# A gate projection in products of 256 moving columns in place of 512, in a fused two-layer block on one Trainium2 core

## The chip, the core and the metric

The kernel runs on one core of a Trainium2 chip. The core has a matrix engine (TensorE, PE in the profile; its weight loads are shown apart as PEld), a vector engine (VectorE, DVE), a scalar engine (ScalarE, ACT), GpSimd (POOL) and SyncE (SP), which issues the transfers from the chip's memory. A product of TensorE has a stationary operand (the weights in the array, up to 128x128), which a weight load brings in, and a moving operand, whose columns stream past it; the result is added up in a PSUM bank. The metric is the device time of one execution in microseconds (us), lower is better.

## What is computed

A first layer block (a convolution branch, a gated recurrence and a per-layer embedding with a gate) is followed by a second one (dilated attention, retention). All inputs are float32; there are 512 tokens of 2048 features. The part that the change concerns is the gate near the end of the first block:

```python
def first_block(x, p, norm_mix_g, w_in, ..., w_ple_gate, w_ple_proj, final_norm_g):
...
        m = jax.nn.sigmoid(ga) * (ya @ w_a_out[i]) + jax.nn.sigmoid(gb) * (yb @ w_b_out[i])
        x = x + m @ w_o[i]

        gate = jax.nn.sigmoid(rmsnorm(x, ple_norm_g[i]) @ w_ple_gate[i])
        x = x + gate * (p[i] @ w_ple_proj[i])

    return rmsnorm(x, final_norm_g)
```

`w_ple_gate` is 2048 x 2048, and x is 512 x 2048. The second block starts with another norm and its own input projection.

## The kernel before, in words

**Layout.** Activations are kept transposed, features on the 128 partitions and the 512 tokens along the row, as 16 k-tiles of 128 x 512. Every dense projection computes, for each group of 512 output features, four output tiles of 128 features x 512 tokens, each in a PSUM bank of its own (128 x 512 float32 fills a bank).

**Three products per tile pair.** To keep float32 accuracy with the reduced type `fp32r`, both operands are split in a high and a low part: WH and WL for the weights, XH and XL for the activations. Each k-tile of each output tile takes three products into the same bank: XH with WH, XL with WH, and XH with WL. In the names of the profile, `bank<-XL,WH` is the product with moving XL and stationary WH. So the stationary operand of the first two products is the same. ScalarE makes the high part from the loaded weights (line 395), VectorE the low part (line 418), units of two k-tiles at a time. SyncE loads the units (`load_unit`, line 453) through four buffers `RAW`; `WH` and `WL` have three buffers each.

**The program `pe`.** It walks through all projections in a fixed order and calls `pe_dense` for each group; the products come from line 366. The gate projection, `("gate", g)` for g in 0 to 3, has 16 k-tiles in each group. It comes behind `("proj", g)` (moving PH and PL) and ahead of `("qr", 0)`, the first projection of the second block. With `fed=True` the products of the first k-tile are ordered by part (XH,WH of all four tiles, then XL,WH, then XH,WL), since the activations are just being made; the others go three by three.

**Signals.** Every engine's program is written out with semaphores. The first product of a tile waits for its weights, its activations, and the bank's last reader; the last product of a tile signals `dense`, on which ScalarE waits for the sigmoid of the gate (line 2111, `GT<-bank`). VectorE multiplies with the projected embedding and adds to x (lines 2508 and 2512). The last product of a unit signals too, and frees the weights' buffers for line 395.

**Other work on TensorE that the argument uses.** Line 467 sums with a matrix of ones, in full float32; lines 472 and 473 do it in `fp32r` with two products; line 1943 sums four pieces of 128 columns in full float32. Lines 782 and 798 are small products of the recurrence, of 32 stationary columns. In the last output group, line 366 has products of 384 moving columns (`cols=EARLY`), with the names KEPT_H and KEPT_L for kept weights.

Of the kernel before, what the change touches and what calls it, by code (L numbers as in the profile page):

```python
# [107 lines left out]
def idle(n):  # L108
    for _ in range(n):
        yield  # L110
# [84 lines left out]
for _name, _w, _r, _nk, _c in GROUPS:  # L195
    FIRST[_name] = len(UNITS)
    for _k in range(0, _nk, 2):
        _row = _r + (_k + 8) % 16 * 128 if _name[0] == "out" else _r + _k * 128
        UNITS.append((_w, _row, _c))
EARLY, LATE = slice(0, 384), slice(384, 512)  # L200
NKEPT = 5
KEPT = range(FIRST["out", 3], FIRST["out", 3] + NKEPT)
LASTU = range(FIRST["out", 3], len(UNITS))
# [21 lines left out]
def build(nc, xT, pT, vec, logits, cst, masks, ident, w_in, w_a, w_b, w_o, w_gate, w_proj,  # L225
# [6 lines left out]
    def sb(name, shape, dt, at):  # L232
        return nc.alloc_sbuf_tensor_at(name, [128] + shape, dt, offset=base + at)
# [4 lines left out]
    XH = sb("XH", [16, 512], F32R, 40960)  # L238
    XL = sb("XL", [16, 512], F32R, 73728)
# [10 lines left out]
    W0 = C0 + 3680 + 4 * NVEC  # L250
    KEPT_H = sb("KEPT_H", [NKEPT, 2, 512], F32R, W0 + 32768)
    KEPT_L = sb("KEPT_L", [NKEPT, 2, 512], F32R, W0 + 53248)
    GB = sb("GB", [2, 512], F32, W0 + 90112)
# [24 lines left out]
    bank = [nc.alloc_psum_tensor(f"bank{i}", [128, 512], F32) for i in range(8)]  # L278
# [46 lines left out]

    pe_turns, act_turns, dve_turns, sp_turns = Turns(), Turns(), Turns(), Turns()

    def pe_dense(name, xh, xl, ready, swap=False, kmap=None, fed=False, cols=slice(0, 512)):
        nk = NK[name]
        mine = take(4, 0, NDENSE)  # L330
        banks[name] = mine
        gone = [held[b] for b in mine]
        for i, b in enumerate(mine):
            held[b] = (free_by(name), (name, i))
        for k in range(nk):
            n = FIRST[name] + k // 2
            wh, wl = high_of(n), low_of(n)
            if fed and k == 0:
                work = [(0, i, (j,)) for j in range(3) for i in range(4)]
            elif fed and k == 1:  # L340
                work = [(1, i, (0, 1, 2)) for i in range(4)]
            else:
                work = [(k - k % 2 + j, i + k % 2 * 2, (0, 1, 2)) for i in range(2) for j in range(2)]
            for q, i, parts in work:
                kk = kmap[q] if kmap else q
                b = mine[i]
                c = slice(i * 128, i * 128 + 128)
                if swap:
                    pairs = [(xh[:, kk, c], wh[:, q % 2]), (xl[:, kk, c], wh[:, q % 2]),
                             (xh[:, kk, c], wl[:, q % 2])]  # L350
                else:
                    pairs = [(wh[:, q % 2, c], xh[:, kk]), (wh[:, q % 2, c], xl[:, kk]),
                             (wl[:, q % 2, c], xh[:, kk])]
                for j in parts:
                    l, r = pairs[j]
                    if j == 0:
                        T.wait_ge(hi, (yield hi, n if n or q else "first"))
                        T.wait_ge(xhi, (yield xhi, (ready, kk)))
                        if q == 0 and gone[i]:
                            T.wait_ge(gone[i][0], (yield gone[i]))  # L360
                    if j == 1:
                        T.wait_ge(xlo, (yield xlo, (ready, kk)))
                    if j == 2:
                        T.wait_ge(lo, (yield lo, n if n or q else "first"))
                    first, final = q == 0 and j == 0, q == nk - 1 and j == 2
                    ins = nc.tensor.matmul(bank[b][:, cols], l, r[:, cols], start=first, stop=final)  # L366
                    done = [(name, i)] * (j == 2 and q == nk - 1)
                    done += [("unit", n)] * (j == 2 and k % 2 == 1 and (q, i) == work[-1][:2])
                    if done:
                        ins.then_inc(dense.sem, dense.step(*done))  # L370
            if name[0] == "z" and k == 15:
                pe_turns.rest(2)
            yield from pe_turns.after_step()
# [1462 lines left out]
    def pe():  # L1836
        shared[0] = True
        turns = pe_turns
        T.wait_ge(dve, (yield dve, "ones"))
        for n in range(11):  # L1840
            nc.tensor.matmul(bank[7][:, 0:128], ONES, ONES, start=True, stop=True)  # L1841
        turns.specials.append(start_part("pe", None, norm0_pe()))
        yield from pe_dense(("fl", 0), XH1, XL1, "raw", fed=True)
        yield from turns.finish(turns.specials)
        for half in range(2):
            if half:
                yield from pe_dense(("fl", 1), XH, XL, "h")
                yield from turns.finish(turns.specials)
            yield from pe_dense(("q", half), XH, XL, "h", fed=not half)
            shared[0] = False  # L1850
            yield from pe_dense(("iv", half), XH, XL, "h", swap=True)
            for i in range(4):
                turns.specials.append(hgrn_pe(i, 4 * half + i))
            for name in ("cg", "xa", "bg", "za"):
                yield from pe_dense((name, half), XH, XL, "h")
        yield from pe_dense(("og", 0), XH, XL, "h")
        yield from pe_dense(("og", 1), XH, XL, "h")
        yield from turns.finish(turns.specials)
        turns.specials.append(idle(8))
        for g in range(4):  # L1860
            yield from pe_dense(("ga", g), XH, XL, "h")
            if g == 0:
                turns.pace = 1.2
            yield from pe_dense(("wa", g), YH, YL, "ya")
        for g in range(4):
            yield from pe_dense(("gb", g), XH, XL, "h")
            if g == 3:
                yield from turns.finish(turns.specials)
                turns.pace = 1.0
                shared[0] = True  # L1870
                turns.specials.append(idle(16))
            yield from pe_dense(("wb", g), YH, YL, "o", fed=True)
        for g in range(4):
            yield from pe_dense(("wo", g), XH, XL, "m", fed=g == 0)
        for g in range(4):
            yield from pe_dense(("proj", g), PH, PL, "p")
            if g == 0:
                b, was = special_bank("r_ple", dve, ("r_ple", "m"))
                T.wait_ge(was[0], (yield was))
                T.wait_ge(pool, (yield pool, ("acc1", 15)))  # L1880
                ones_sum(b, AC[:, 0], ("r_ple", "sum"))
                turns.specials.append(idle(16))
        for g in range(4):
            yield from pe_dense(("gate", g), XH, XL, "g", fed=True)
        turns.specials.append(second_norm_pe())
        yield from pe_dense(("qr", 0), XH, XL, "xg")
        yield from turns.finish(turns.specials)
        yield from pe_dense(("kr", 0), XH, XL, "h2")
        shared[0] = False
        for half in range(2):  # L1890
            yield from pe_dense(("vr", half), XH, XL, "h2", swap=True)
        left = set(range(4))
        for r in range(4):
            turns.specials.append(retention_pe(r, left))
        heads = set(range(8))
        for half in range(2):
            yield from pe_dense(("qa", half), XH, XL, "h2")
            while half and left:
                yield from turns.piece(turns.specials)
            yield from pe_dense(("ka", half), XH, XL, "h2")  # L1900
            yield from pe_dense(("va", half), XH, XL, "h2", swap=True)
            for i in range(4):
                turns.specials.append(attention_pe(4 * half + i, heads))
        turns.specials.append(last_values_pe(heads))
        for zb in ZBASE:
            yield from pe_dense(("z", zb), XH, XL, "h2")
            while zb < 8 and any(zb <= h < zb + 4 for h in heads):
                yield from turns.piece(turns.specials)
            if zb == 4:
                yield from turns.finish(turns.specials)  # L1910
        shared[0] = True
        for b in (7, 6):
            age.remove(b)
            age.insert(2, b)
        for g in range(3):
            yield from pe_dense(("out", g), XH, XL, "y", kmap=KORDER, fed=True)
        yield from pe_dense(("out", 3), XH, XL, "y", kmap=KORDER, fed=True, cols=EARLY)
        turns.specials.append(idle(2))
        turns.specials.append(early_norm_pe())
        yield from late_dense_pe()  # L1920
        yield from late_norm_pe()
# [852 lines left out]
```

## Time and profile before

| | |
|---|---|
| median of 3 runs | 2510.56 us (2510.26 to 2510.63) |
| span of the profiled execution, first to last instruction | 2508.7 us |
| TensorE (PE) busy | 2502.2 us, 12614 products, and as many weight loads |
| VectorE busy | 1358.9 us |
| ScalarE busy | 918.4 us |
| granted TensorE clock, mean | 1.000 |
| moved by DMA | 317.95 MB, mean 127 GB/s |

Spans are of one profiled execution, which has a time of its own; the runs give the time from outside, and the two differ by what lies before the first and behind the last instruction. A busy share near 100% on TensorE tells that it always has a product under way, not that each product is cheap: the records of neighbouring products overlap, since a product is still draining while the next one streams. What one costs is read from the distance between two starts. Idle time of an engine that nobody waits for costs nothing.

### The profile page before, as it was taken

To read this page: it belongs to the slowest core of one execution; us is meant where nothing else is said; L and a number is where in the kernel's file an instruction comes from. 1 tells how busy PE (TensorE), PEld (TensorE's weight loads), DVE (VectorE), ACT (ScalarE), POOL (GpSimd) and SP (SyncE) were. 2 spreads that over 40 slices of the span, in tenths; PEclk is the share of its full clock that TensorE was granted. 3 is DMA by queue.
4 is the path that set the end of the run, shared out by engine and by line. 5 is a ranking of instruction groups with operands and counts; after the bars stand their busy time and mean duration, and the time that the engine had idled before them with its cause. 6 is when DMAs were issued, how large, how long until landed. Compare 5 with 4: busy or idle time off the path is not lost.

```text
span 2508.7 us, 31305 instructions
## 1 busy us (share of the span) xinstructions
PE 2502.2 (100%) x12614; PEld 2075.9 (83%) x12614; DVE 1358.9 (54%) x2248; ACT 918.4 (37%) x1259; POOL 149.5 (6%) x195
## 2 busy tenths in 40 slices
PE   9999999999999999999999999999999999999999
PEld 8888888888888888888888888888888888888888
DVE  7557744567544555655443363485256555665425
ACT  6633325333332222322232253443344344544423
POOL 0011110012100000000001103200000000000001
PEclk9999999999999999999999999999999999999999
DMA  5333333333335666666443232236222243433432
GB/s 192 110 96 95 96 105 95 95 95 100 100 93 164 213 218 214 218 212 212 149 161 110 93 101 93 93 101 178 92 76 76 85 125 101 113 106 112 178 101 101
DMA packets 213633, 317.95 MB, mean 127 GB/s; under 512 B 66736, under 2 KB 69680, under 8 KB 212464
## 3 DMA queue, kind: packets, MB, share of 16 engines
q1 hardware_dynamic: 208592, 312.55, 40.2%
q0 software_dynamic: 4320, 2.99, 0.5%
q8 instruction: 99, 1.62, 0.3%
q10 hardware_dynamic: 576, 0.42, 0.1%
q14 instruction: 46, 0.38, 0.1%
HBM read 295.43 MB, written 8.39 MB: 121 GB/s over the span
## 4 chain that ended last, share of the span: by engine, by line
PE 100%; ACT 0%; DVE 0%; issue 0%; ACTq 0%; DVEq 0%
PE bank L366 94%; PE bank L1449 1%; PE bank L1450 1%; PE bank L1451 1%; PE bank L798 0%; PE bank L857 0%; PE bank L782 0%; PE bank L860 0%; PE bank L825 0%; PE bank L1841 0%; PE bank L1955 0%; PE bank L1953 0%; PE bank L1954 0%; PE bank L467 0%; ACT OT L2266 0%; PE bank L472 0%
## 5 line engine op out<-in xcount | busy, mean ns | idle before, releaser
L366 PE MATMUL bank<-XH,WH 128*128 128x512 f32 (+1 forms) x2776 | 1078.7, 390 | 0.0
L366 PE MATMUL bank<-XH,WL 128*128 128x512 f32 (+1 forms) x2776 | 1074.5, 389 | 0.0
L366 PE MATMUL bank<-XL,WH 128*128 128x512 f32 (+1 forms) x2776 | 1074.0, 389 | 0.0
L418 DVE TENSOR_TENSOR WL<-RAW,WH 128x1024 fp32r<-128x1024 f32 x430 | 530.1, 1234 | 760.6 <-ACT WH L395 760.0
L395 ACT CAST WH<-RAW 128x1024 fp32r<-128x1024 f32 x430 | 450.1, 1048 | 1113.4 <-PE bank L366 1102.2
L366 PEld LDWEIGHTS bank<-XH,WL 128*128 128x128 f32 x2776 | 521.0, 188 | 108.1 <-DVE WL L418 0.2
L366 PEld LDWEIGHTS bank<-XH,WH 128*128 128x128 f32 x2776 | 521.0, 188 | 107.7 <-ACT WH L395 0.2
L366 PEld LDWEIGHTS bank<-XL,WH 128*128 128x128 f32 x2776 | 521.2, 188 | 107.1 <-issue 0.5
L366 PE MATMUL bank<-WH,XL 128*128 128x512 f32 x384 | 149.4, 389 | 0.0
L366 PE MATMUL bank<-WH,XH 128*128 128x512 f32 x384 | 149.4, 389 | 0.0
L366 PE MATMUL bank<-WL,XH 128*128 128x512 f32 x384 | 149.4, 389 | 0.0
L1234 DVE CUSTOM_DVE_ANT_0 AST<-AST,CB 128x512 f32<-128x512 f32 x192 | 125.1, 685 | 10.0 <-DMA AST<-in_w_ada 9.8
L366 PE MATMUL bank<-YH,WH 128*128 128x512 f32 x256 | 97.7, 389 | 0.0
L366 PE MATMUL bank<-YH,WL 128*128 128x512 f32 x256 | 97.6, 389 | 0.0
L366 PE MATMUL bank<-YL,WH 128*128 128x512 f32 x256 | 97.6, 389 | 0.0
L366 PEld LDWEIGHTS bank<-WH,XH 128*128 128x128 f32 x384 | 72.1, 188 | 15.1
L366 PEld LDWEIGHTS bank<-WL,XH 128*128 128x128 f32 x384 | 72.1, 188 | 14.9
L366 PEld LDWEIGHTS bank<-WH,XL 128*128 128x128 f32 x384 | 72.1, 188 | 14.9
L2597 POOL TENSOR_TENSOR AC<-AC,GT 128x512 f32<-128x512 f32 x15 | 22.7, 1512 | 748.0 <-ACT GT L2087 746.4
L366 PEld LDWEIGHTS bank<-YL,WH 128*128 128x128 f32 x256 | 48.0, 188 | 10.0
L366 PEld LDWEIGHTS bank<-YH,WL 128*128 128x128 f32 x256 | 48.0, 188 | 10.0
L366 PEld LDWEIGHTS bank<-YH,WH 128*128 128x128 f32 x256 | 48.1, 188 | 10.0
(351 smaller groups left out, 1882.7 us busy)
## 6 DMA issues: line engine op xcount, KB each, us to landing
RAW<-in_w_in SPq DMA_DIRECT2D x303, 512.0 KB, 3.8
AST<-in_w_ada SPq DMA_DIRECT2D x192, 256.0 KB, 4.1
RAW<-in_w_o SPq DMA_DIRECT2D x32, 512.0 KB, 3.7
RAW<-in_w_gate SPq DMA_DIRECT2D x32, 512.0 KB, 3.6
RAW<-in_w_out SPq DMA_DIRECT2D x32, 512.0 KB, 3.7
RAW<-in_w_a SPq DMA_DIRECT2D x16, 512.0 KB, 4.2
RAW<-in_w_b SPq DMA_DIRECT2D x16, 512.0 KB, 4.3
PT<-ZT SPq DMA_DIRECT2D x256, 32.0 KB, 1.9
```

Source lines behind the costliest of these rows:

```text
L366: ins = nc.tensor.matmul(bank[b][:, cols], l, r[:, cols], start=first, stop=final)
L395: nc.scalar.copy(high_of(m), RAW[:, m % NRAW]).then_inc(hi.sem, hi.step(m))
L418: nc.vector.tensor_tensor(low_of(m), RAW[:, m % NRAW], high_of(m).bitcast(F32), ALU.subtract).then_inc(lo.sem, lo.step(m))
L1234: nc.vector.tensor_tensor_reduce(AST[:, n % 3], AST[:, n % 3], CB[:, q % 2], 1.0, 0.0, ALU.mult, ALU.add, PART[:, n:n + 1]).then_inc(dve.s ...
L1449: nc.tensor.matmul(b, high, right_high, start=start, stop=False)
L1450: nc.tensor.matmul(b, high, right_low, start=False, stop=False)
L1451: return nc.tensor.matmul(b, low, right_high, start=False, stop=stop)
L2597: nc.gpsimd.tensor_tensor(AC[:, 0], AC[:, 0], GT[:, j % 4], ALU.add).then_inc(pool.sem, pool.step(("acc1", j)))
```

## The change

`pe_dense` gets an argument `halves`. Where it is given, each product is issued as two, one for tokens 0 to 255 and one for tokens 256 to 511, into the two halves of the same bank, with the same stationary operand. Only the gate projection passes it. The waits ahead of a product stand ahead of the first half, and signals are on the second. Of the very first product of a bank only the first half has `start`. All other projections, and the work of the other engines, are as before.

```diff
--- before.py
+++ after.py
@@ -198,6 +198,7 @@
 EARLY, LATE = slice(0, 384), slice(384, 512)
+TOKEN_HALVES = slice(0, 256), slice(256, 512)
 NKEPT = 5
@@ -325,7 +326,7 @@
-    def pe_dense(name, xh, xl, ready, swap=False, kmap=None, fed=False, cols=slice(0, 512)):
+    def pe_dense(name, xh, xl, ready, swap=False, kmap=None, fed=False, cols=slice(0, 512), halves=None):
         nk = NK[name]
@@ -363,7 +364,12 @@
                     first, final = q == 0 and j == 0, q == nk - 1 and j == 2
-                    ins = nc.tensor.matmul(bank[b][:, cols], l, r[:, cols], start=first, stop=final)
+                    if halves:
+                        for h, part in enumerate(halves):
+                            ins = nc.tensor.matmul(bank[b][:, part], l, r[:, part], start=first and h == 0, stop=final,
+                                                   skip_group_check=True)
+                    else:
+                        ins = nc.tensor.matmul(bank[b][:, cols], l, r[:, cols], start=first, stop=final)
                     done = [(name, i)] * (j == 2 and q == nk - 1)
@@ -1881,7 +1887,7 @@
         for g in range(4):
-            yield from pe_dense(("gate", g), XH, XL, "g", fed=True)
+            yield from pe_dense(("gate", g), XH, XL, "g", fed=True, halves=TOKEN_HALVES)
```

On TensorE, where the gate projection begins, before (PH and PL are the moving operands of the projection ahead; the four XH products in a row are the first k-tile of the four output tiles):

```order
6275 L366 MATMUL bank<-PH,WL 128x512
6276 L366 MATMUL bank<-XH,WH 128x512 x4
6277 L366 MATMUL bank<-XL,WH 128x512 x4
6278 L366 MATMUL bank<-XH,WL 128x512 x4
6279 L366 MATMUL bank<-XH,WH 128x512
6280 L366 MATMUL bank<-XL,WH 128x512
6281 L366 MATMUL bank<-XH,WL 128x512
```

The same place in the changed kernel, where the products of the gate have moved to line 369 and all others to line 372:

```order
6275 L372 MATMUL bank<-PH,WL 128x512
6276 L369 MATMUL bank<-XH,WH 128x256 x8
6277 L369 MATMUL bank<-XL,WH 128x256 x8
6278 L369 MATMUL bank<-XH,WL 128x256 x8
6279 L369 MATMUL bank<-XH,WH 128x256 x2
6280 L369 MATMUL bank<-XL,WH 128x256 x2
6281 L369 MATMUL bank<-XH,WL 128x256 x2
```

Nothing has changed places; each product has become two in a row.

## Rows read from the trace of the kernel before

**Rows 1.** The page: span, PE's busy time, and its clock in 40 slices
```profile
span 2508.7 us, 31305 instructions
...
PE 2502.2 (100%) x12614; PEld 2075.9 (83%) x12614; DVE 1358.9 (54%) x2248; ACT 918.4 (37%) x1259; POOL 149.5 (6%) x195
...
PEclk9999999999999999999999999999999999999999
```
**Rows 2.** The page: the chain that ended last, by engine and by line
```profile
PE 100%; ACT 0%; DVE 0%; issue 0%; ACTq 0%; DVEq 0%
PE bank L366 94%; PE bank L1449 1%; PE bank L1450 1%; PE bank L1451 1%; PE bank L798 0%; PE bank L857 0%; PE bank L782 0%; PE bank L860 0%; PE bank L825 0%; PE bank L1841 0%; PE bank L1955 0%; PE bank L1953 0%; PE bank L1954 0%; PE bank L467 0%; ACT OT L2266 0%; PE bank L472 0%
```
**Rows 3.** Busy time of each engine in the gate stage
```profile
core 0: us, PE busy (x) PEld busy (x) DVE busy (x) ACT busy (x) POOL busy (x), PEclk, DMA share, GB/s
1461.10:1635.20 174.10, 174.10 (x769) 144.15 (x768) 83.47 (x100) 71.45 (x96) 34.72 (x22) 1.00 0.30 97
```
**Rows 4.** Line 366 in that stage: duration ns min/median/max, starts; and who waited
```profile
L366 PE MATMUL bank<-XH,WH x256: 389/389/390, 1461.1 to 1634.5; 128*128 128x512 f32 x128
...
  ACT WH L395: 93.8, 28
```
**Rows 5.** Timeline (start us, us, engine): the stage's two ends
```profile
1461.13 0.84 PE L366 MATMUL bank<-XH,WH 128*128 128x512 f32 x3
...
1635.21 0.39 PE L366 MATMUL bank<-XH,WH 128*128 128x512 f32 x1
```
**Rows 6.** Timeline inside the gate stage: products and loads at 512 columns
```profile
1499.89 0.39 PE L366 MATMUL bank<-XH,WH 128*128 128x512 f32 x1
...
1500.12 0.39 PE L366 MATMUL bank<-XL,WH 128*128 128x512 f32 x1
1500.12 0.19 PEld L366 LDWEIGHTS bank<-XH,WL 128*128 128x128 f32 x1
1500.35 0.39 PE L366 MATMUL bank<-XH,WL 128*128 128x512 f32 x1
...
1503.97 0.39 PE L366 MATMUL bank<-XH,WH 128*128 128x512 f32 x1
```
**Rows 7.** Timeline of the last output group: products and loads at 384 columns
```profile
2459.75 0.33 PE L366 MATMUL bank<-XH,KEPT_H 128*128 128x384 f32 x1
...
2459.93 0.19 PEld L366 LDWEIGHTS bank<-XH,KEPT_L 128*128 128x128 f32 x1
...
2460.10 0.19 PEld L366 LDWEIGHTS bank<-XH,KEPT_H 128*128 128x128 f32 x1
...
2463.91 0.33 PE L366 MATMUL bank<-XH,KEPT_H 128*128 128x384 f32 x1
```
**Rows 8.** Timeline: eight float32 products of 128 columns, and the return to line 366
```profile
1677.79 1.05 PE L1943 MATMUL bank<-ONES_R,BQ 128*128 128x128 f32 x8
...
1678.57 0.19 PEld L366 LDWEIGHTS bank<-XH,WH 128*128 128x128 f32 x1
...
1678.68 0.19 PEld L366 LDWEIGHTS bank<-XL,WH 128*128 128x128 f32 x1
1678.91 0.39 PE L366 MATMUL bank<-XL,WH 128*128 128x512 f32 x1
```
**Rows 9.** Timeline: a load behind a wait of the sequencer
```profile
1844.59 0.19 PEld L472 LDWEIGHTS bank<-TQ,ONES_R 128*128 128x128 f32 x1 [0.20 <-issue]
...
1844.94 0.39 PE L473 MATMUL bank<-TQ,ONES_R 128*128 128x512 f32 x1
```
**Rows 10.** Second loads of WH, for XL, on line 366: busy us, mean ns
```profile
L366 PEld LDWEIGHTS bank<-XL,WH 128*128 128x128 f32 x2776 | 521.2, 188 | 107.1 <-issue 0.5
```
**Rows 11.** Timeline of the loads of line 467: float32 products of 512 columns
```profile
1651.97 0.19 PEld L467 LDWEIGHTS bank<-AC,ONES_R 128*128 128x128 f32 x1 [0.24 <-issue]
...
1652.82 0.19 PEld L366 LDWEIGHTS bank<-XH,WH 128*128 128x128 f32 x1 [0.24 <-ACT WH L395]
```
**Rows 12.** Timeline: small products of the recurrence
```profile
148.74 0.73 PE L798 MATMUL bank<-XX 128*32 128x16 f32 x64
```

## The prediction

> **What bounds the kernel now.** I read the first two parts of the page first. TensorE (PE) is busy 2502.2 of 2508.7 us, VectorE 54% and ScalarE 37%, and the clock digit of PE is 9 in every slice [rows 1]. The chain of work that ended last is PE for 100% of the span, 94% of it on line 366, the product that this change edits [rows 2]. So only what a product costs PE moves the time. Next I cut out the stage that is changed. The gate projection is 4 groups x 16 k-tiles x 4 output tiles x 3 products = 768 products, 256 of each of the three kinds, of which one kind's row stands in [rows 4]. Its first product starts at 1461.13 and the first of the next projection at 1635.21 [rows 5]. That is 174.08 us, or 226.7 ns from one start to the next, on average. The granted clock is 1.00 there (the 2.4 GHz level) and PE is busy for all of it [rows 3]. The mean duration of a product, 389 ns, is not its price: products overlap in the pipeline, and PE is charged by the distance between starts. The timeline shows the same distance without a hole: 18 steps from 1499.89 to 1503.97, 226.7 ns each [rows 6].
>
> **What a product is charged for.** Two widths stand in the trace with the same operand type. At 512 columns it is 226.7 ns. At 384 columns (last output group) 24 steps from 2459.75 to 2463.91 give 173.3 ns [rows 7]. The difference, 53.4 ns for 128 columns, is 0.417 ns per column, one column per cycle of 2.4 GHz. What is left is 226.7 - 213.3 = 13.4 ns at 512 and 173.3 - 160.0 = 13.3 ns at 384: a fixed amount that each product pays, whatever its width.
>
> Each product also has its own weight load, shown with 188 ns. It isn't serial with the products, nor is 188 ns its occupancy: in [rows 7] one load follows another every 173 ns, less than it "takes". In [rows 6] the load for the next product starts together with the current product (1500.12 and 1500.12), so it has one product's time to finish. How short that can be is seen where the next load follows at once: 1678.57 to 1678.68, 110 ns, and the product behind it starts 0.23 us after that, so both load and product were through at the normal rate [rows 8].
>
> **The change, part by part.**
>
> Removed: 768 products of 512 columns, 768 x 226.7 ns = 174.1 us.
>
> Added: 1536 products of 256 columns. Each streams 256 x 0.417 = 106.7 ns and, by the law of [rows 6, 7], pays 13.3 ns: 120.0 ns. A pair costs 240.0 ns in place of 226.7, so +13.3 ns per old product. Sum: 768 x 13.3 ns = **+10.2 us**, all on the path, since PE has no idle time in the stage to put it in.
>
> Added: 768 weight loads with the weights that are already there. Nothing suggests that the second is skipped: in the kernel before, the products of XH and XL with the same WH follow each other, and and the one of XL loads it again, 2776 times [rows 10]; and the product behind such a repeated load starts no earlier than any other (XL at 1500.12, 0.23 us behind 1499.89, as the next with new weights at 1500.35) [rows 6]. The question is whether a load still hides behind a product of only 120.0 ns. With 110 ns [rows 8] it does, with 10 ns to spare. This is the narrowest cover of the whole sum, and no row has a run of `fp32r` products closer than 173 ns, so it gets bounds from the nearest rows. Upper end: in [rows 9] the sequencer had waited, the load started at 1844.59, and the second product started 0.35 us later, at 1844.94; less one step of 0.227 that is 0.12 us from start of load to effective start of its product, so up to 123 ns with the rounding: 2 x 123 - 226.7 = +19.3 ns, +14.8 us. Lower end: the shortest spacing of full-array products in the trace is that of [rows 8]: eight of 128 columns, in 32-bit float at half rate (512 columns take two steps of 0.425 us from 1651.97 to 1652.82 [rows 11], 0.83 ns per column, so 128 take 106 ns, as much streaming as 256 of ours). They start 7 steps apart over 1677.79 to 1678.57, 111.4 ns each: 2 x 111.4 - 226.7 = -3.9 ns, -3.0 us. I take 120.0, because the two rows of the same operand type and the same line lie exactly on one straight line, and the row for the lower end is another type.
>
> Issuing 1536 more instructions: at most one product and one load per 120 ns. In [rows 12] 64 small products, each with a load of its own, are through in 0.73 us, 11 ns each. So this costs nothing.
>
> Waits and signals: they sit on the same places as before, on the first half of a pair and on its second half. PE waits for nothing new. ScalarE and VectorE, which split the weights, are busy 71.45 and 83.47 of the 174.10 us [rows 3], and ScalarE waits for PE 28 times, 93.8 us in all [rows 4]. They follow PE, and get 10 us more room. No engine is late behind the stage, and since PE never waits there, their room gives nothing back. The tail is not touched.
>
> The sum on the profiled execution: 2508.7 + 10.2 = 2518.9 us. The median of the runs, 2510.56, is 1.9 us more than that span, so the forecast is 2510.56 + 10.2 = **2520.8 us**; the gate stage goes from 174.1 to 184.3 us.
>
> **Rivals.**
>
> A, the load sets the pace: if from load to product takes 123 to 126 ns once the product in front is short, the pair costs 246 to 252 ns and the time is 2510.56 + 768 x (19.3 to 25.3 ns) = 2525 to 2530 us. For it: the 0.12 us of [rows 9], and a margin of only 10 ns. Against it: the 110 ns of [rows 8]. Up to 124.7 ns it stays inside my range.
>
> B, not slower: the 13.3 ns belong to a change of weights and not to a product, and the second half, with the same weights, goes without. Then the pair takes 226.7 ns and the time is 2510.6. It decides in favour of "no change" from a pair of 233 ns down. Against it stands the repeated WH of [rows 6], which pays in full.
>
> C, the fixed amount is small for short products: with the 111.4 ns of the lower end it is -3.0 us, 2507.6, at 115 ns still +2.5. For it speaks that the 32-bit products of [rows 8] pay only about 5 ns. Against: they have another type, and 384 columns show no less than 512. The Trainium skill ("TensorE: Matmul & The Clock Gate", section "Back-to-back issue gap") gives an isolated warm product N/2.4 + 2.5 ns; by that rule the change would cost one more 2.5 ns per old product, 768 x 2.5 = 1.9 us as an estimate. This trace does not agree with that rule for its products: it would be 215.8 at 512 columns, where 226.7 is measured.
>
> D, the shown 188 ns is what a load occupies once nothing hides it: 2 x 188 - 226.7 = 149.3 ns, +114.7 us, 2625 us. Against: the 173 ns of [rows 7] and the 110 of [rows 8]. A stream of 256 columns at the half rate of [rows 11] would be as far off: 2 x 215 - 226.7 = 203 ns, +156 us. At 384 columns there is no sign of it.
>
> E, the change doesn't do what it says: the listing has 128x256 x2 where 128x512 stood. What could fail is only a drop of the second load; the pair would still stream 213.3 ns and pay for two products between 0 and 26.7 ns, which is B or the forecast.
>
> **How the numbers follow.** Forecast (118 to 122 ns per product, 2518 to 2524): 0.71. A: 0.10, of which 0.03 ends above 2528. B: 0.05. C: 0.07, of which 0.04 within 0.2% and 0.03 just above it. D: 0.06. E is counted in B and the forecast, and 0.01 is left for a real gain. A measurement of this kernel can tell about 0.2%, 5 us, from no change. Slower by over that: 0.71 + 0.10 + 0.03 + 0.06 = 0.90. Within it: B and the rest of C, 0.09. Faster: 0.01. The range reaches from 2515 (+4.4 us, a pair of 232.5 and a spacing of 116.2 ns) to 2528 (+17.4 us, 249.4 and 124.7 ns). It takes in the upper bound of +14.8 us, and leaves out B (0.05), the lower part of C (0.04), the top of A (0.03), D (0.06) and the real gain (0.01), 0.19 together; the lower bound of -3.0 us is among what is left out.
>
> **What would show it.** In the profile after: line 366 splits, the gate part has 1536 products of 128x256 with 1536 loads; starts 120 ns apart, both from half to half and from pair to pair; the stage 184.3 us long; clock 1.00; no idle row of PE. If starts alternate between 107 and 120 ns, B holds. If load follows load at 123 ns or more and the product starts right when a load ends, A holds. Unequal spacing with instruction issue named as the releaser would mean that issue costs something after all. The forecast is wrong if the fixed 13.3 ns are not a matter of the product count.

## The result, and the profile after

| | before | after |
|---|---|---|
| median of the runs, us | 2510.41 (2509.98 to 2510.63, 4 runs) | 2520.73 (2519.98 to 2522.0, 4 runs) |
| ratio | | 1.0042, 95% interval 1.0026 to 1.0058 |
| span of the profiled execution, us | 2508.7 | 2520.7 |
| gate stage, us | 174.1 | 184.3 |
| distance between two starts there, ns | 226.7 | 120.0 |

The kernel is 10.3 us slower, 0.4%, where +10.2 us and 2520.8 us were forecast. The page of the changed kernel answers to [rows 1]:

```profile
span 2520.7 us, 32841 instructions
...
PE 2513.2 (100%) x13382; PEld 2117.0 (84%) x13382; DVE 1359.1 (54%) x2248; ACT 918.5 (36%) x1259; POOL 149.3 (6%) x195
```

There are 768 more products and 768 more weight loads; VectorE and ScalarE have as many instructions as before, and their busy time is the same to 0.2 us. The stage itself, its ends in the timeline (as in [rows 5]) and its busy time (as in [rows 3]):

```profile
1462.87 1.12 PE L369 MATMUL bank<-XH,WH 128*128 128x256 f32 x8
...
1647.18 0.40 PE L372 MATMUL bank<-XH,WH 128*128 128x512 f32 x1
```

```profile
core 0: us, PE busy (x) PEld busy (x) DVE busy (x) ACT busy (x) POOL busy (x), PEclk, DMA share, GB/s
1462.80:1647.20 184.40, 184.40 (x1539) 184.36 (x1538) 84.10 (x100) 71.45 (x96) 34.46 (x22) 1.00 0.30 93
```

1647.18 - 1462.87 = 184.31 us, 10.2 us more than the 174.08 of [rows 5], at the same granted clock. By it, 184.31 / 1536 = 120.0 ns from start to start. The weight loads were busy for 144.15 us of the stage in [rows 3]; now it is all of it, 184.36. That looks like an engine that has become the bound, but this figure can't show it: a load is shown with 192 ns, longer than the distance to the next one, so the records overlap. (That the loads don't set the pace follows from the quarters below, where they come every 111.6 ns.) Inside the stage (as in [rows 6]; each row is a pair of halves):

```profile
1486.62 0.40 PE L369 MATMUL bank<-XH,WH 128*128 128x256 f32 x2
1486.74 0.31 PEld L369 LDWEIGHTS bank<-XL,WH 128*128 128x128 f32 x2
1486.86 0.40 PE L369 MATMUL bank<-XL,WH 128*128 128x256 f32 x2
...
1487.10 0.40 PE L369 MATMUL bank<-XH,WL 128*128 128x256 f32 x2
```

Pairs start 0.24 us apart, whether the weights change (XL,WH to XH,WL) or not (XH,WH to XL,WH). From half to half inside a pair it is the same 0.12: a row's 0.40 is one distance plus one product of 0.283.

How long its loads and products are shown (ns, min/median/max), and who waits for the products, in the view of line 369:

```profile
L369 PEld LDWEIGHTS bank<-XL,WH x512: 192/192/192, 1463.7 to 1646.7; 128*128 128x128 f32 x171
...
L369 PE MATMUL bank<-XH,WL x512: 283/283/283, 1464.8 to 1647.1; 128*128 128x256 f32 x171
...
  ACT WH L401: 102.7, 28
```

ScalarE waits 102.7 us there in place of the 93.8 of [rows 4], 8.9 us more in the same 28 waits: the stage's extra time is handed on as idle time to an engine that nobody waits for.

**The span grew by 12.0 us, not 10.2.** The rest is ahead of the stage, which starts at 1462.87 and not at 1461.13, 1.74 us later. Most of it is one wait near the start, on the squares of the first norm. Before, and below it after, in the timeline:

```profile
38.32 0.30 PEld L467 LDWEIGHTS bank<-SC,ONES_R 128*128 128x128 f32 x2 [0.21 <-DVE SC L569]
```

```profile
40.15 0.30 PEld L473 LDWEIGHTS bank<-SC,ONES_R 128*128 128x128 f32 x2 [1.46 <-DVE SC L575]
```

Nothing is changed there. The spans of the other three executions of the changed kernel are 2518.7 to 2519.7 us, so this belongs to the execution and not to the change.

### The profile page after: what moved, and what is told of

It reads as the page before. It is cut to its first block, busy times and chain, and to the rows that moved or that the text cites. A ratio compares the mean times of both kernels' runs of the same rounds, so it can differ in the third digit from the quotient of the medians.

```text
span 2520.7 us, 32841 instructions
## 1 busy us (share of the span) xinstructions
PE 2513.2 (100%) x13382; PEld 2117.0 (84%) x13382; DVE 1359.1 (54%) x2248; ACT 918.5 (36%) x1259; POOL 149.3 (6%) x195
## 4 chain that ended last, share of the span: by engine, by line
PE 98%; DMA 1%; DVE 0%; issue 0%; ACT 0%; SPq 0%; ACTq 0%; DVEq 0%
PE bank L372 86%; PE bank L369 7%; PE bank L1457 1%; PE bank L1455 1%; PE bank L1456 1%; DMA RAW<-in_w_in 1%; PE bank L804 0%; PE bank L863 0%; PE bank L788 0%; DVE SC L575 0%; PE bank L866 0%; PE bank L831 0%; PE bank L473 0%; PE bank L1961 0%; PE bank L1960 0%
## 5 line engine op out<-in xcount | busy, mean ns | idle before, releaser
L372 PE MATMUL bank<-XH,WH 128*128 128x512 f32 x2520 | 980.8, 390 | 0.0
L372 PE MATMUL bank<-XH,WL 128*128 128x512 f32 x2520 | 976.7, 389 | 0.0
L372 PE MATMUL bank<-XL,WH 128*128 128x512 f32 x2520 | 976.4, 389 | 0.0
L372 PEld LDWEIGHTS bank<-XH,WL 128*128 128x128 f32 x2520 | 473.1, 188 | 98.1 <-DVE WL L424 0.2
L372 PEld LDWEIGHTS bank<-XH,WH 128*128 128x128 f32 x2520 | 473.2, 188 | 97.5 <-issue 0.2
L372 PEld LDWEIGHTS bank<-XL,WH 128*128 128x128 f32 x2520 | 473.1, 188 | 97.0 <-issue 0.5
L369 PE MATMUL bank<-XL,WH 128*128 128x256 f32 x512 | 101.2, 283 | 0.0
L369 PE MATMUL bank<-XH,WL 128*128 128x256 f32 x512 | 101.2, 283 | 0.0
L369 PE MATMUL bank<-XH,WH 128*128 128x256 f32 x512 | 101.2, 283 | 0.0
L369 PEld LDWEIGHTS bank<-XH,WH 128*128 128x128 f32 x512 | 79.1, 192 | 0.1
```

Source lines behind the costliest of these rows:

```text
L369: ins = nc.tensor.matmul(bank[b][:, part], l, r[:, part], start=first and h == 0, stop=final, skip_group_check=True)
```

## Experiments

Time is given as the median, or as one run where there was one. The distance between starts is read in each from one row of the view of the product's line: for two products per tile, the first XH,WL product is number 17 of 1536 and the last is number 1536, so the row's range holds 1519 distances; for four products, number 33 of 3072, 3039 distances; for one, number 9 of 768, 759 distances. In the changed kernel that is (1647.1 - 1464.8) / 1519 = 120.0 ns. Where single distances are given below, they come from the start times of the records in the kept trace. The code cuts show the main lines of an edit; `...` stands for what is left out.

### All of the first half, then all of the second

```diff
-                for j in parts:
+                for h, j in [(h, j) for h in range(len(halves or (cols,))) for j in parts]:
                     l, r = pairs[j]
+                    part = (halves or (cols,))[h]
...
```

> The gate stage still issues 1536 products of 256 columns, but all three of the first half of the tokens come before the three of the second half, so nearly every second load brings in other weights than the one before it. Theory (each product pays about 13.3 ns whatever its weights): starts 120.0 ns apart, stage 184.3 us, 2520.7 us in all. Rival (a load of weights that are already there is cheaper, so the changed kernel's repeated loads kept its price low): spacing above 120 ns, up to 123, stage up to 189 us, 2525 us.

```profile
L370 PE MATMUL bank<-XH,WL x512: 282/283/284, 1464.0 to 1646.3; 128*128 128x256 f32 x171
```

2520.52 us (5 runs), ratio to before 1.0040, interval 1.0025 to 1.0054; 182.3 / 1519 = 120.0 ns. So the changed kernel doesn't owe its 120.0 ns to the repeated weights: loads of new weights hide as well. Whether a repeated load is cheaper can't be seen here, since at 120 ns a load hides in either case; the quarters below show that it isn't.

### The other projections too

```diff
     def pe_dense(name, xh, xl, ready, ..., cols=slice(0, 512), halves=None):
+        halves = TOKEN_HALVES if cols == slice(0, 512) else None
```

> All dense products of 512 columns, not only the gate's, are issued as two halves: 10272 products in the whole kernel. Theory (13.3 ns for each): +136.9 us, 2647.3 us, spacing 120.0 ns everywhere. Rival (the two split parts of the price do not add up elsewhere, as other engines had been waited for or have waits that this hides): clearly less than 130 us more. Rival (more instructions than the issue can bring on): clearly more than 140 us.

```profile
L370 PE MATMUL bank<-XH,WL x5504: 279/283/283, 7.8 to 2591.3; 128*128 128x256 f32 x197
...
149.78 0.40 PE L370 MATMUL bank<-XH,WL 128*128 128x256 f32 x2
150.02 0.40 PE L370 MATMUL bank<-XH,WH 128*128 128x256 f32 x2
```

2645.38 us (4 runs) beside 2510.53 of before, ratio 1.0537 (1.0520 to 1.0555): +134.9 us for 10272 products, 13.1 ns each, where 13.3 were expected. The price adds up over the kernel at 13.4 times the dose, in stages with little and with much other work. Comparing the two timelines point by point, 1.65 of the missing 2 us gather between 148 and 660 us, where the small products of the recurrence interrupt the dense products 32 times, about 0.05 us at each; why an interruption costs less there was not looked into.

### A split of 384 and 128

```diff
-TOKEN_HALVES = slice(0, 256), slice(256, 512)
+TOKEN_HALVES = slice(0, 384), slice(384, 512)
```

> Each gate product is issued as two, of 384 and of 128 columns. The columns streamed and the number of products are as in the changed kernel. Theory with the load as a second limit (spacing is the larger of columns/2.4 + 13.3 ns and some 111 ns that a weight load needs): 173.3 + 111 = 284 ns a pair, stage 218.4 us, 2554.7 us. Rival (only the fixed amount and the columns count): 240.0 ns a pair, stage 184.3 us, 2520.7 us. If short products stream at a lower rate, the pair takes clearly more than 284 ns.

```profile
L369 PE MATMUL bank<-XH,WL x512: 222/306/391, 1463.8 to 1681.6; 128*128 128x384 f32 x86, 128*128 128x128 f32 x85
```

2556.55 us. 217.8 / 1519 = 143.4 ns on average, 287 ns a pair, where the load theory had 284 and the mere sum of columns and fixed amounts 240. Same columns, same number of products, 36 us slower than the halves: behind the short product there isn't time enough to load the next weights. The records fit this, but not by their start times alone: the short product starts 228 ns behind the long one, and the next long one 58 ns behind the short one. The long one is shown with 391 ns, though, where a product of 384 columns has 0.33 us in [rows 7], so it seems to start in the record before its weights are there, and to wait some 57 ns under its own name. In an uneven pair the single distance is thus not a product's price; only the sum of the pair is. A lower streaming rate of short products would cost more than these 3 ns.

### Four products of 128 columns, with 128 and with 64 stationary columns

```diff
-TOKEN_HALVES = slice(0, 256), slice(256, 512)
+TOKEN_HALVES = tuple(slice(128 * i, 128 * i + 128) for i in range(4))
```

> Each gate product is issued as four of 128 columns. Theory (the weight load, some 111 ns, becomes the limit): 4 x 111 = 444 ns, stage 341 us, 2677 us. Rival (only fixed amount and columns): 4 x 66.7 = 266.7 ns, stage 204.8 us, 2541 us. If short products stream at a lower rate, spacing is clearly above 111 ns.

```profile
L369 PE MATMUL bank<-XH,WL x1024: 272/276/278, 1465.4 to 1804.7; 128*128 128x128 f32 x171
```

2679.92 us. 339.3 / 3039 = 111.6 ns, although a quarter streams only 53.3 ns. Of the four loads in a row, at least three bring in weights that are already there, and the timeline has:

```profile
1500.14 0.53 PEld L369 LDWEIGHTS bank<-XH,WL 128*128 128x128 f32 x4
```

That is three distances and one load of 0.192 us, 0.11 us from one to the next; over the stage, the mean distance behind each of the four lies between 111 and 112.2 ns. So here, where the load sets the pace, a repeated load costs as much as a new one: it is neither skipped nor cheaper. To show that this is the load's time and no property of short products, the same with half of the weights:

```diff
-ins = nc.tensor.matmul(bank[b][:, part], l, r[:, part], ...
+ins = nc.tensor.matmul(bank[b][0:64, part], l[:, 0:64], r[:, part], ...
```

> Four products of 128 columns each, with 64 stationary columns in place of 128 (half of the gate's output features left out). Theory (the 111.6 ns floor of the quarters is the time to load 128 columns): the load takes about half, and the spacing falls to 53.3 + 13.3 = 66.7 ns, stage 204.8 us, 2541 us; if the fixed amount goes with the load's size, 60 ns, stage 184.3 us. Rival (the floor belongs to short products, whatever is loaded): spacing stays at 111.6 ns, stage 343 us, 2680 us.

```profile
L369 PE MATMUL bank<-XH,WL x1024: 220/222/224, 1463.6 to 1646.0; 128*64 128x128 f32 x171
```

2521.07 us. 182.4 / 3039 = 60.0 ns. The floor falls by nearly half with the weights, so it is the load. (The edit also halves the output of each product. But 128 and 240 moving columns with full weights, below, have the same 111.6 to 111.7 ns with outputs of different size, which speaks for the load.) But 60.0 is not the 66.7 of the theory either: only 6.7 ns are left over the 53.3 of streaming.

### Whole products with 64 stationary columns

The edit is the last one with `TOKEN_HALVES = (slice(0, 512),)`.

> The gate products are whole again (512 columns), but with 64 stationary columns in place of 128, so that half of the gate's output features is left out. Theory (the 13.3 ns are fixed for a product of this type): spacing 226.7 ns, stage 174.1 us, 2510.4 us. Rival (the 13.3 ns are lost to the weight load that runs beside the product, and go with its size): 220.0 ns, stage 169.0 us, 2505.3 us.

```profile
L369 PE MATMUL bank<-XH,WL x256: 387/390/397, 1463.6 to 1638.1; 128*64 128x512 f32 x128
```

2513.1 us. 174.5 / 759 = 229.9 ns, which neither expectation had: half of the weights, and 16.6 ns over streaming in place of 13.3. It isn't one amount either: the distances repeat sequences such as 224, 226, 235, 230, 235, 230 ns, where the changed kernel has 119 or 120 throughout but for the first; the cause was not looked into. So the fixed amount is not lost in proportion to the load beside the product.

### Just below 256 columns

```diff
-TOKEN_HALVES = slice(0, 256), slice(256, 512)
+TOKEN_HALVES = slice(0, 272), slice(272, 512)
```

> Each gate product is issued as two, of 272 and of 240 columns, so that one lies below 256. Theory (spacing is columns/2.4 + 13.3 ns while that is above some 111 ns): 126.7 and 113.3 ns, 240.0 ns a pair, stage 184.3 us, 2520.7 us. Rival (products of fewer than 256 columns stream more slowly): the 240-column product takes more, up to 200 + 13 ns at half rate, and the stage grows by up to 77 us. Rival (the load needs 120 ns): 126.7 + 120 = 246.7 ns a pair, stage 189.5 us.

```profile
L369 PE MATMUL bank<-XH,WL x512: 269/280/293, 1464.1 to 1643.3; 128*128 128x272 f32 x86, 128*128 128x240 f32 x85
```

2518.41 us. 179.2 / 1519 = 118.0 ns on average, 236 a pair, 4 less than the lowest expectation. No slower streaming under 256 columns, and no load of 120 ns; on the contrary the pair is cheaper than two equal halves. To see whether it is the narrower one, two of 240 columns:

```diff
-TOKEN_HALVES = slice(0, 256), slice(256, 512)
+TOKEN_HALVES = slice(0, 240), slice(240, 480)
```

> Two products of 240 columns each; the last 32 of the 512 tokens are left out of the gate. Theory (columns/2.4 + 13.3 ns while above the load's floor of 111.6): 113.3 ns each, stage 174.1 us, 2510.4 us. Rival, after the 118.0 ns mean of 272 and 240 columns (the fixed amount shrinks where the load has just enough time): at most 111.6 ns each, stage 171.4 us or less, 2507.7 us or less; 109.3 ns would be 167.9 us and 2504.2 us.

```profile
L369 PE MATMUL bank<-XH,WL x512: 272/274/278, 1463.0 to 1632.6; 128*128 128x240 f32 x171
```

2507.64 us. 169.6 / 1519 = 111.7 ns: the load's floor of the quarters, and less than the 113.3 that columns and fixed amount give. So 13.3 ns is not paid at 240 columns. By how much the amount is lower can't be read, since the floor hides it. Nor is it all of the 4 ns: if a product of 240 columns takes 111.7 ns in the uneven pair too, 124.3 are left for that of 272, 11.0 over its streaming of 113.3. How the pair shares its saving is not shown.

### The operand type

```diff
+    def as_bf16(t):
+        return t.bitcast(mybir.dt.bfloat16)[:, 1::2]
...
-ins = nc.tensor.matmul(bank[b][:, part], l, r[:, part], ...
+ins = nc.tensor.matmul(bank[b][:, part], as_bf16(l), as_bf16(r)[:, part], ...
```

With whole products (`TOKEN_HALVES = (slice(0, 512),)`):

> The gate products are whole again (512 columns), but both operands are read as bfloat16 (the upper halves of the same numbers), so the gate is less exact. Theory (the 13.3 ns belong to the operand type fp32r, as the 32-bit float products pay only some 2 to 5 ns): spacing near 216 ns, stage 165.7 us, 2502 us. Rival (they belong to any product that has a load of its own): spacing 226.7 ns, stage 174.1 us, 2510.4 us.

In the timeline of this kernel:

```profile
1499.74 0.39 PE L372 MATMUL bank<-XH,WH 128*128 128x512 bf16 x1
...
1499.96 0.10 PEld L372 LDWEIGHTS bank<-XH,WL 128*128 128x128 bf16 x1
...
1501.09 0.39 PE L372 MATMUL bank<-XH,WH 128*128 128x512 bf16 x1
```

2509.56 us. Six steps in 1.35 us, 225.0 ns. The load is shown with 0.10 us in place of 0.19, but the product pays 11.7 ns over streaming, nearly what `fp32r` pays. And in halves:

> The gate products in halves of 256 columns, both operands read as bfloat16. If the fixed amount belongs to fp32r: about 109 ns if the load of 128 bfloat16 columns takes less, stage 168 us, 2504 us; or the 111.6 ns floor if the load takes as long as in fp32r, stage 171.4 us, 2507.7 us. Rival (fixed amount for any product with a load): 120.0 ns, stage 184.3 us, 2520.7 us.

```profile
L372 PE MATMUL bank<-XH,WL x512: 273/274/275, 1463.7 to 1635.9; 128*128 128x256 bf16 x171
```

2510.84 us, beside 2510.2 of before (one run of each). 172.2 / 1519 = 113.4 ns. In this type the split costs hardly anything: 2 x 113.4 - 225.0 = 1.8 ns per old product, 1.4 us, because the amount over streaming is 6.7 ns at 256 columns and 11.7 at 512. Here too it isn't fixed. The operands are read with a step of two elements; packed ones were not tried.

## Why the prediction was right, point by point

- **Only PE's price counts.** The stage grew by 10.2 us and the median by 10.3. ScalarE took 8.9 us of it as waiting time, and VectorE's busy time in the stage went only from 83.47 to 84.10 us.
- **Streaming and fixed amount, 106.7 + 13.3 = 120.0 ns.** Measured 120.0, and by the start times in the trace no distance is off by more than a nanosecond but the stage's first, 114 ns. This term was right in size. Its reason, a fixed amount "whatever its width", was too strong: it is 13.3 ns at 256, 384 and 512 columns of `fp32r` with 128 stationary columns, but at most 11.7 at 240, 6.7 at 128 with 64 stationary columns, and 16.6 at 512 with 64. The prediction argued that the two rows "lie exactly on one straight line", but two points always do. What they did show is a slope of one column per cycle and one amount at two widths, and nothing below 384. That 256 lies on the line was the value taken, and the two widths around it, 272 and 240, don't both: by the same sum their pair would have cost 240.0 ns, and it took 236. To this extent the exact hit was luck.
- **The load hides, with some 10 ns to spare.** Right, and the margin is 120.0 - 111.6 = 8.4 ns. The 110 ns of [rows 8] were the right row; the upper bound of 123 ns from [rows 9] was not met (rival A). The quarters and the split of 384 and 128 show what happens without that cover.
- **The repeated load is neither skipped nor cheaper** (rival B). The pair takes 240.0 ns and not 226.7, with the same 120 from half to half and from pair to pair; and in the quarters, where nothing hides a load, the repeated ones come 111 to 112 ns apart like the new ones.
- **Rival C, a small amount for short products,** was wrong for the change and right for its neighbourhood: 240 columns reach the load's floor, and bfloat16 has 6.7 ns at 256. The Trainium skill's 2.5 ns per product ("TensorE: Matmul & The Clock Gate", section "Back-to-back issue gap") was met nowhere in the gate's products: even bfloat16 took 225.0 ns at 512 columns, where N/2.4 + 2.5 gives 215.8 as an estimate. The Trainium skill gives that rule for isolated products, and none here is. By the Trainium skill's rule for a load ("TensorE: Matmul & The Clock Gate", section "LDWEIGHTS (loading the stationary operand)"), P/1.2 with P columns, 128 columns take 106.7 ns as an estimate; the measured floor is 111.6, 5 ns more. For 64 columns the rule gives 53.3 ns, and the measured 60.0 leaves room for it.
- **Rival D** was ruled out, as each of its two forms needs over 2600 us.
- **Issue costs nothing.** With nearly all dense products in halves, 10272 products and loads more, the distance stays 120.0 ns.
- **From span to median.** The prediction put 1.9 us outside the profiled span. In each execution of the changed kernel time and span differ by 1.3 us (2522.0 and 2520.7 in the profiled one). The other 0.6 us was a difference between executions of the kernel before. It didn't change the forecast, which added the price to the median.

What stays open is the cause of the amount over streaming. It doesn't shrink with the load's size at 512 columns (16.6 ns with half of the weights), and isn't a constant of the product. With bfloat16 it is much smaller at 256 columns (6.7 against 13.3) and a little at 512 (11.7), but that run also read its operands with a step of two, so type and step aren't told apart. And no run has a product without a load of its own: the 13.3 ns are the price of a product together with its load, and which of the two they belong to is not shown. The runs give the amount at several points and no rule.

## What to carry to other kernels

Where TensorE never waits, read the distance between two starts, not the duration: subtract the streaming of the columns, and what is left is the price of one more product, provided that it is the same at the new width. In `fp32r` it was, and the cut at 256 columns cost 13.3 ns. In bfloat16 11.7 ns were left at 512 columns, and the cut cost 1.8. For the load to stay hidden, each piece has to take longer than its neighbour's weight load, here some 112 ns; pieces of 256 columns do, and pieces of 240 are at that floor. One piece far below it costs the difference on top, even if its partner is long. A line through two measured widths is a good guess for the next width, but its constant has to be tested there before more is built on it.

## What was not expected of the hardware

- Two products of 272 and 240 columns take 236 ns, two of 256 take 240 ns, for the same columns.
- With 64 stationary columns a product of 512 columns takes 229.9 ns, 3 ns more than with 128, and single distances vary from 224 to 236 ns.
- A load of 128 columns is shown with 188 ns in `fp32r`, 192 once loads follow each other within 120 ns, and about 96 ns in bfloat16; the distance that it enforces in `fp32r` is 111.6 ns. The shown duration was no guide to it.
